# Key-value and mid-state products from hi and lo parts, with inner products between them and the state updates moved

## The reference

```
q, k, v, g = split(rms_norm(x) @ w_in); q, k = rotary(q), rotary(k) * 256 ** -0.5
scores = (q @ k.T) * decay_mask                  # within a chunk, causal
inner  = scores @ v
cross  = (q @ s_prev) * cross_decay              # s_prev: the state of the chunks before
kv     = (k * k_decay).T @ v                     # key-value product, 256 x 512
s_new  = gamma ** L * s_prev + kv                # for the prompt, and for each of 8 samples
o = group_norm(inner + cross)
x = x + (silu(g) * o) @ w_out
```

## Time and profile before

| | |
|---|---|
| median of 3 runs | 1457.37 us (1456.34 to 1457.72) |
| the profiled execution | 1458.02 us |
| its span in the profile | 1454.7 us |
| mean granted TensorE clock | 1.00 |
| TensorE busy | 1449.2 us, 100% |
| VectorE busy | 799.9 us, 55% |
| ScalarE busy | 543.2 us, 37% |
| GpSimd busy | 2.9 us |
| DMA | 171.94 MB, mean 118 GB/s |

### The profile page before, as it was taken

One profiled execution on the slowest core, in us unless ns is written; L12 is line 12 of the kernel. 1 busy time (PEld: TensorE's weight loads), 2 busy tenths in 40 slices (PEclk: granted clock), 3 DMA queues, 4 the chain that ended last, 5 costly groups with the idle time before them and its releaser, 6 DMA issues.

```text
span 1454.7 us, 27349 instructions
## 1 busy us (share of the span) xinstructions
PE 1449.2 (100%) x11428; PEld 1395.2 (96%) x11428; DVE 799.9 (55%) x1066; ACT 543.2 (37%) x776; POOL 2.9 (0%) x24
## 2 busy tenths in 40 slices
PE   9999999999999999999999999999999999999998
PEld 9699789879979999999999999999999999999998
DVE  7885577468458855555542427444565555553222
ACT  5552273264155543333331314222343333332222
POOL 0000000000000000000000000000000000000000
PEclk9999999999999999999999999999999999999999
DMA  8445253463444322222222222232223222222221
GB/s 302 149 186 192 96 225 107 180 232 104 166 162 178 115 89 87 89 98 87 87 93 100 87 88 88 88 97 92 89 89 100 87 87 99 88 87 101 92 88 59
DMA packets 47742, 171.94 MB, mean 118 GB/s; under 512 B 5608, under 2 KB 6248, under 8 KB 46624
## 3 DMA queue, kind: packets, MB, share of 16 engines
q1 hardware_dynamic: 47488, 170.76, 33.8%
q0 software_dynamic: 32, 0.03, 0.0%
q10 hardware_dynamic: 144, 0.00, 0.0%
HBM read 149.44 MB, written 21.55 MB: 118 GB/s over the span
## 4 chain that ended last, share of the span: by engine, by line
issue 100%; POOL 0%; POOLq 0%
POOLq L107 0%; POOL ident L266 0%; POOL h_tail L263 0%; POOL k_tail_stack L275 0%; POOL mean_v L259 0%; POOL ident L257 0%; POOL h_hi L261 0%; POOL h_lo L262 0%; POOL sample_ones L274 0%; POOL sample_ones L279 0%; POOL mean_d L258 0%; POOL late_q_decayed L276 0%; POOL seed L268 0%; POOL seed L269 0%; POOL seed L271 0%
## 5 line engine op out<-in xcount | busy, mean ns | idle before, releaser
L846 ACT ACTIVATE w_hi<-w_raw 128x1024 fp32r<-128x1024 f32 x227 | 240.1, 1059 | 671.4 <-PE ps L405 469.1
L405 PE MATMUL ps<-h_hi,w_hi 128*128 128x264 f32 (+2 forms) x2300 | 468.3, 285 | 0.4 <-DVE h_lo L1184 0.4
L405 PE MATMUL ps<-h_lo,w_hi 128*128 128x264 f32 (+2 forms) x2300 | 465.4, 284 | 0.0
L405 PE MATMUL ps<-h_hi,w_lo 128*128 128x264 f32 (+2 forms) x2300 | 464.9, 283 | 0.0
L1159 DVE TENSOR_TENSOR w_lo<-w_raw,w_hi 128x1024 fp32r<-128x1024 f32 x227 | 277.0, 1222 | 334.5 <-ACT w_hi L846 334.2
L405 PEld LDWEIGHTS ps<-h_hi,w_hi 128*128 128x128 f32 x2300 | 355.8, 188 | 1.5 <-issue 0.8
L405 PEld LDWEIGHTS ps<-h_hi,w_lo 128*128 128x128 f32 x2300 | 355.5, 188 | 0.0
L405 PEld LDWEIGHTS ps<-h_lo,w_hi 128*128 128x128 f32 x2300 | 355.3, 188 | 0.0
L695 PE MATMUL ps<-z_hi,w_lo 128*128 128x264 f32 (+1 forms) x704 | 144.7, 283 | 0.0
L695 PE MATMUL ps<-z_lo,w_hi 128*128 128x264 f32 (+1 forms) x704 | 144.6, 283 | 0.0
L695 PE MATMUL ps<-z_hi,w_hi 128*128 128x264 f32 (+1 forms) x704 | 144.6, 283 | 0.0
(11 more groups left out here) (205 smaller groups left out, 1407.7 us busy)
## 6 DMA issues: line engine op xcount, KB each, us to landing
w_raw<-in_w_units_dram SPq DMA_DIRECT2D x227, 512.0 KB, 3.3
states<-in_state_ret_dram SPq DMA_DIRECT2D x32, 512.0 KB, 8.5
out_ret_s_dram<-states SPq DMA_DIRECT2D x32, 512.0 KB, 4.6
v_bcast<-v_scratch SPq DMA_DIRECT2D x8, 1024.0 KB, 5.6
x_res<-in_x_all_dram SPq DMA_DIRECT2D x8, 268.0 KB, 6.0
out_ret_p_dram<-tmp SPq DMA_DIRECT2D x4, 512.0 KB, 3.7
out_y_prompt_dram<-y_rows SPq DMA_DIRECT2D x4, 512.0 KB, 2.6
decay<-in_decay_dram SPq DMA_DIRECT2D x4, 299.5 KB, 3.8
```

The costliest lines, as they stand in the source:

```text
L405: out = mm(PS[:, 2 * s + half, at:at + n_col], a, b[:, lo:lo + n_col], start=first and n == 0, stop=last and n == 2)
L846: fn(WH[:, c % NS, :], RAW[:, c % NR, :], ACT.Copy).then_inc(hi_ready, 1)
```

## The change

- The key-value products are computed from three fp32r products each. ACT writes the high part of V beside V (all four blocks, L1017 and L1018) and the high part of the keys (`k_rows_hi`); DVE subtracts to get both low parts (L1416, L1425, `k_rest`). DVE no longer scales two V blocks itself.
- The products of the late queries with the mid state become three fp32r products each. ACT copies the mid state's high part (`mid_hi`), DVE writes the low part (`mid_rest`), and the late queries are split likewise.
- TensorE's order: the mid sums for e = 0 and 1, then the early inner products of dt = 0, which wait for two score tiles, then the rest of the key-value products and the mid queries of dt = 0 by turns, then the late part of dt = 0, then dt = 1 to 3. Tile dt = 2 waits for the first of two additions that make up `KV`.
- The state updates, with ACT's outer products, move into the stages p = 1, 2, 3 of the output projection (2, 2 and 4 of them). Those of the last head move into the first two bodies of the FFN of layer 0.
- SP's list: the broadcast of V waits for the inner products and stands behind unit 14; the next head's units 0 to 5 come before or between the state stores. y_sample leaves from ACT instead of GpSimd.
- Some SBUF tiles lie over others: the mid state parts and the V parts in space that is free at that time, `KV` in the gate tile.

The diff, cut to what the text speaks of:

```diff
+UPDATES = ((), (0, 1), (2, 3), (4, 5, 6, 7))
+FFN_UPDATES = ((0, 1, 2, 3), (4, 5, 6, 7))
...
-                VB = sb("v_bcast", [P, NB, DV], scope=s3)
+                VH = sb("v_rows_hi", [P, 4, DV], F32R, scope=s3)
+                VL = sb("v_rows_lo", [P, 4, DV], F32R, scope=s3)
...
+            def store_state(h, b):
+                sp.wait_ge(s_upd, NB * h + (b + 1))
+                sp.dma_start(st_out[b, h], S[:, b, :]).then_inc(s_out[b], 16)
...
-                for b in range(NB):
-                    sp.wait_ge(s_upd, NB * h + (b + 1))
-                    sp.dma_start(st_out[b, h], S[:, b, :]).then_inc(s_out[b], 16)
-                for n in range(14, 16):
...
+                sp.wait_ge(v_sent, 16 * h + 16)
+                sp.wait_ge(inner_done, 4 * h + 4)
+                for half in range(2):
+                    b = half * NB // 2
+                    sp.dma_start(VB[:, b:b + NB // 2, :], VSCR[b:b + NB // 2, :].partition_broadcast(P)).then_inc(vb_in[half], 16)
+                in_heads(h, 15)
+                for n in range(4):
...
+                        ffn_in_unit(0, 1, n)
...
+                    for p in (1, 2):
+                        for b in UPDATES[p]:
+                            store_state(h, b)
+                        next_unit(h, 3 + p)
...
+                def key_value(e, js):
+                    for j in js:
+                        kh, kl = KNH[:, j, e * P:(e + 1) * P], KNL[:, j, e * P:(e + 1) * P]
+                        for q, (k, v) in enumerate(((kh, VH), (kh, VL), (kl, VH))):
+                            out = mm(PS[:, 6 + e, :], k, v[:, j, :], start=j in (0, 2) and q == 0, stop=j == 1 and q == 2)
+                    return out
+
+                for e in range(2):
+                    pe.wait_ge(kn_lo, 4 * h + 2 * e + 2)
+                    pe.wait_ge(v_lo, 4 * h + 4)
+                    key_value(e, (0, 1)).then_inc(mid_done, 1)
+
+                def key_value_end(e):
+                    pe.wait_ge(mid_lo, 2 * h + e + 1)
...
+                def early_values(dt):
+                    for j in range(2):
...
+                def mid_queries(dt, e):
+                    pe.wait_ge(ql_lo, 2 * h + e + 1)
+                    pe.wait_ge(mid_lo, 2 * h + e + 1)
+                    km = slice(e * DV + dt * P, e * DV + (dt + 1) * P)
+                    for q, (k, c) in enumerate(((KMH, QLH), (KMH, QLL), (KML, QLH))):
+                        mm(PS[:, 2 * INNER[dt] + 1, 0:N_LATE + NB], k[:, km], c[:, e, :], start=e == 0 and q == 0, stop=False)
...
+                pe.wait_ge(p_ready, 5 * h + 2)
+                pe.wait_ge(const_ready, QL_ZERO)
+                early_values(0)
+                key_value_end(0)
+                mid_queries(0, 0)
+                key_value_end(1).then_inc(kv_done, 1)
+                mid_queries(0, 1)
                 pe.wait_ge(p_ready, 5 * h + 5)
...
+                late_values(0).then_inc(inner_done, 1)
+                for dt in range(1, 4):
...
-                        pe.wait_ge(kv_ready, h + 1)
+                        pe.wait_ge(kv_sum, h + 1)
...
+                    early_values(dt)
                     for e in range(2):
...
+                        mid_queries(dt, e)
+                    late_values(dt).then_inc(inner_done, 1)
...
-                for b in (0, 2):
...
+                for b in range(4):
+                    if b < 3:
+                        act.wait_ge(v_acc, 3 * h + b + 1)
+                    else:
+                        act.wait_ge(unit_done, U_HEAD * h + (NS + 8))
                     fn(V[:, b, :], PS[:, 2 + b, :], ACT.Copy, scale=RN[:, b:b + 1]).then_inc(v_ready, 1)
...
+                    fn(VH[:, b, :], PS[:, 2 + b, :], ACT.Copy, scale=RN[:, b:b + 1]).then_inc(v_hi, 1)
...
-                    fn(KN[:, j, :], src, ACT.Copy, scale=DEC[:, DEC_ROW + j:DEC_ROW + j + 1]).then_inc(kn_ready, 1)
+                    fn(KNH[:, j, :], src, ACT.Copy, scale=DEC[:, DEC_ROW + j:DEC_ROW + j + 1]).then_inc(kn_ready, 1)
...
+                def mid_hi(e):
+                    act.wait_ge(mid_done, 2 * h + e + 1)
+                    fn(KMH[:, e * DV:(e + 1) * DV], PS[:, 6 + e, :], ACT.Copy).then_inc(mid_ready, 1)
+
+                mid_hi(0)
+                for e in range(2):
+                    act.wait_ge(ql_ready, 2 * h + e + 1)
+                    fn(QLH[:, e, 0:N_LATE], QT[:, e, :], ACT.Copy).then_inc(ql_hi, 1)
+                mid_hi(1)
...
-                for e in range(2):
-                    act.wait_ge(mid_done, 2 * h + e + 1)
-                    fn(KM[:, e * DV:(e + 1) * DV], PS[:, 6 + e, :], ACT.Copy).then_inc(mid_ready, 1)
...
+                    if not last:
+                        for b in UPDATES[p]:
+                            outer(h, b)
...
+            act.wait_ge(ys_out, 1)
+            act.dma_start(io["y_sample"], YS[:].rearrange("p k b -> p (k b)")).then_inc(ys_sent, 16)
...
+            def update(h, b):
+                dve.wait_ge(samp_kv, 16 * h + (2 * b + 2))
+                at = (b % 2) * 1024
+                stt(S[:, b, :], S[:, b, :], DEC[:, DEC_STATE:DEC_STATE + 1], G[:, at:at + 1024], ALU.mult, ALU.add).then_inc(s_upd, 1)
...
-                dve.wait_ge(v_acc, 3 * h + 2)
-                ts(V[:, 1, :], PS[:, 3, :], RN[:, 1:2], None, ALU.mult).then_inc(v_some, 1)
...
+                for b in range(4):
+                    dve.wait_ge(v_ready, 5 * h + b + 2)
+                    dve.wait_ge(v_hi, 4 * h + b + 1)
+                    tt(VL[:, b, :], V[:, b, :], VH[:, b, :].bitcast(F32), ALU.subtract).then_inc(v_lo, 1)
+                    if b < 2:
+                        dve.wait_ge(v_tail, 4 * h + 4)
+                        tt(QT[:, b, :], Q[:, b, CUT:TP], DEC[:, DEC_Q:DEC_ROW], ALU.mult).then_inc(ql_ready, 1)
...
+                def k_rest(j):
+                    if j % 2 == 0:
+                        dve.wait_ge(kn_ready, 4 * h + j + 2)
+                    src = PS[:, 6 + j // 2, (j % 2) * DK:(j % 2 + 1) * DK]
+                    stt(KNL[:, j, :], src, DEC[:, DEC_ROW + j:DEC_ROW + j + 1], KNH[:, j, :].bitcast(F32),
+                        ALU.mult, ALU.subtract).then_inc(kn_lo, 1)
+
+                k_rest(0)
+                k_rest(1)
...
+                k_rest(2)
+                k_rest(3)
...
+                def mid_rest(e):
+                    dve.wait_ge(mid_ready, 2 * h + e + 1)
+                    mid = slice(e * DV, (e + 1) * DV)
+                    tt(KML[:, mid], PS[:, 6 + e, :], KMH[:, mid].bitcast(F32), ALU.subtract).then_inc(mid_lo, 1)
+
+                mid_rest(0)
...
+                for e in range(2):
+                    dve.wait_ge(ql_hi, 2 * h + e + 1)
+                    tt(QLL[:, e, 0:N_LATE], QT[:, e, :], QLH[:, e, 0:N_LATE].bitcast(F32), ALU.subtract).then_inc(ql_lo, 1)
+                mid_rest(1)
...
-                tt(KV, PS[:, 6:8, :].rearrange("p e v -> p (e v)"), KM, ALU.add).then_inc(kv_ready, 1)
...
+                tt(KV, PS[:, 6:8, :].rearrange("p e v -> p (e v)"), KMH[:].bitcast(F32), ALU.add).then_inc(kv_sum, 1)
+                dve.wait_ge(kv_sum, h + 1)
+                tt(KV, KV, KML[:].bitcast(F32), ALU.add).then_inc(kv_ready, 1)
...
-                dve.wait_ge(s_upd, NB * h + NB)
+                dve.wait_ge(kv_sent, 16 * h + 16)
...
+                    if not last:
+                        for b in UPDATES[p]:
+                            update(h, b)
...
-                body(0, True)
-                with dve.Fori(1, JF // 2) as i:
+                body(0, True, FFN_UPDATES[0] if l == 0 else ())
+                if l == 0:
+                    body(1, False, FFN_UPDATES[1])
```

More of the change, by code:

```diff
@@ L325, in _, with ffn_in_unit, next_unit, head @@
             sp.dma_start(CF[:], io["ffn_consts"]).then_inc(ffn_in, 16)
-            def head(h, first):
-                for n in range(4 if first else 0, 6):
-                    in_heads(h, n)
+            def ffn_in_unit(l, i, n):
+                load(U_FFN_IN[l] + 4 * i + n)
+            def next_unit(h, n):
+                if h < HEADS - 1:
+                    in_heads(h + 1, n)
+                else:
+                    ffn_in_unit(0, 0, n)
+            def store_state(h, b):
+                sp.wait_ge(s_upd, NB * h + (b + 1))
+                sp.dma_start(st_out[b, h], S[:, b, :]).then_inc(s_out[b], 16)
+            def head(h, first, last):
+                def load_state(b):
+                    if not first:
+                        sp.wait_ge(s_out[b], 16 * h)
+                    sp.dma_start(S[:, b, :], st_in[b, h]).then_inc(s_in[b], 16)
+                if first:
+                    for n in range(4, 6):
+                        in_heads(h, n)
                 if first:
@@ L1460, in body @@
                         dve.wait_ge(ff_hi, 2 * i + (JF + 8) * l)
+                    for b in samples:
+                        update(HEADS - 1, b)
                     dve.wait_ge(unit_done, 4 * i + (u0 + NS + 2))
```

192 lines of the change are left out of this document (88 added, 104 removed).

## The result

The changed kernel takes 1448.40 us (median of 6 runs, 1448.32 to 1448.62), the kernel before 1457.24 (6 runs). The ratio is 0.9941, interval 0.9930 to 0.9951. It is faster by 8.8 us; 1449.7 was forecast, 7.7 less, with a range of 1448.0 to 1453.8.

What follows compares the result with a forecast made beforehand. TensorE, busy 1449.2 of 1454.7 us, was taken as the bound. Shorter products -8.1, stall +0.6 and tail -0.2 gave -7.7 from the 1457.37 median: 1449.7 us, range 1448.0 to 1453.8.

Steps and rivals of the forecast that it cites:

- TensorE's sum: Key-value and mid-query products in the heads: 10.68 us becomes 8.66, so 2.02 less a head, 8.1 in four.
- The chain through the mid state: TensorE waits for the mid state's low part: stall 0.6 us in head 0, none in heads 1 to 3.
- The sign named for it: In the profile after, TensorE's waits should list DVE's mid_state_lo with about 0.6 us, mostly in head 0.
- rival B: Mid-state chain late in every head, 0.6 to 1.6 us more in each of four: 1452.1 to 1456.1; chance 0.16.
- The updates moved: State updates moved into output projection and FFN fit in DVE's idle time: cost 0.
- SP's queue: Reordered V broadcast, unit loads, state stores and loads still arrive in time: cost 0.
- Rival C: States' update, store and load end late, the sample fold delays TensorE: 1460.3 us and more; chance 0.03.
- Rival D: No change: DVE late at the z chain returns 2 us a head, 1455 to 1458; chance 0.06.
- The tail: y_sample's transfer leaving from ACT at the end saves 0.2 us, between 0 and 0.67.

Runs made afterwards that it cites:

- a_early_late: Changed kernel with early values of tile 0 (0.64 us) placed behind the rest of the key-value products for e = 0; 1450.36 us.
- a_all32: Changed kernel with key-value and mid-query products as single fp32 products again (rounded parts, low parts not read); 1456.45 us, 0.9996 of before.
- a_upd3: Changed kernel with all eight state updates of heads 0 to 2 behind the split of p = 3; 1448.45 us.
- a_upd1: Changed kernel with all eight state updates of heads 0 to 2 behind the split of p = 1; 1460.47 us.
- a_pool: Changed kernel with y_sample's transfer issued by GpSimd again; 1448.52 us.
- b_act: Kernel before with only y_sample's transfer moved to ScalarE; 1456.87 us against 1456.92.
- a_same: The changed kernel itself, measured again as reference in a later series; 1448.57 us, 0.9942 of before.
- b_gap: Kernel before with only the unused 888-column tile added between z_hi and z_lo of the FFN; 1456.13 us against 1457.02.
- v_late: Changed kernel with late scores x V products (272 and 144 columns) also from three fp32r products each; 1448.91 us.
- v_j2: v_late with the mid state's high and low parts for e = 0 made earlier and the 144-column product single fp32 again; 1447.68 us.

## Why the prediction was right

**TensorE's sum** was right: 2.02 us in a head was forecast, 1.96 came (head 1), and the two halves apart measured 5.1 and 3.0 against 5.2 and 2.9 in four heads. The price of an fp32r product of 280 columns, which no row showed, is 0.129; 0.128 was taken, from a line between two rows. The formula of the Trainium skill, page "TensorE: Matmul & The Clock Gate", section "Back-to-back issue gap", would have given 0.119 and 0.216; the trace has 0.129 and 0.232, so it does not agree, by 7 to 8%. The page has this formula for matmuls back to back, but the section named calls it the gap of an isolated one and gives 0.131 for 512 columns in a sustained stream, from which the trace is further off.

**The chain through the mid state** was right in its place (head 0 alone, TensorE just late) and too long by 0.3: stall 0.26 instead of 0.6. The sign named for it, a row of `mid_state_lo` among TensorE's waits, did not appear, since the stall was too short. The steps held. The operations ahead of mid_rest were each a few hundredths cheaper in a row than the printed durations that the prediction had used, and the block from the second score product on took 67.38 - 65.21 = 2.17 instead of 2.33; mid_rest itself took 0.69 instead of 0.66. 68.8 on the clock of before was forecast for the end of mid_rest, and it came at 68.07 + 0.29 = 68.36. In heads 1 to 3 the cover of 0.2 was 0.3 to 0.4, and rival B had nothing: `a_early_late` shows that 0.64 us less cover costs 0.34 to 0.37 in each.

**The updates moved** cost nothing, as forecast, and `a_all32` and `a_upd3` show it by themselves. `a_upd1` shows that "nothing" holds for the pair at p = 1, not for any number.

**SP's queue**: no transfer among TensorE's waits. Rival C was excluded with over 5 us to spare. Rival D had no ground: in head 1 the first z_lo ended at 220.99 and TensorE wanted it at 223.20, 2.2 us of cover instead of 0.45.

**The tail** was the one term that had no ground: 0.2 taken for ScalarE's issue of y_sample, nothing measured (`a_pool`, `b_act`).

**Not in the forecast** was the place of z_lo, 0.6 us, though the line of the unused tile stood in the full diff. I had read it as a matter of room. With it, the smaller stall (0.3) and no gain in the tail (0.2), -7.7 becomes -8.4, and with the 7.84 that the four heads gave instead of 8.1 it is -8.2. The median moved by 8.3 (`a_same`) to 8.8, depending on the series. It is luck that the sizes which were off within the sum cancel in part: the stall was taken 0.3 too long, the heads' gain 0.3 and the tail's 0.2 too large.

## What to carry to other kernels

Where one engine is busy without a gap, price a replaced instruction by the distance of starts in its own stream, not by its printed duration, and the forecast of its part was good to a few per cent here (2.02 against 1.96). Two fp32 records are worth replacing by three fp32r products while these stay clear of their floor of 0.11 us: here at 512, 280 and 272 columns yes, at 144 no. When a hand-over between engines is new, look for independent work of the waiting engine to put ahead of it: here two products of 0.64 us were worth 1.7 us in four heads.

## What the runs showed of the hardware

- An unused tile in front of z_lo in SBUF changed TensorE's mean distance of starts by 0.3 to 0.8 ns in 121 (`b_gap`), the same to 0.01 us of the stage in every execution that was profiled.
- After a wait of 2.7 us TensorE had a stretch at a granted clock of 0.50 (1.2 GHz) in two heads out of three (`a_upd1`): in head 0 its products slowed down 1.7 us after the wait, in head 2 at once. Each cost some 1.5 us more. In `a_early_late` no such stretch followed the wait of 0.7 us.
- fp32r products with 144 columns cost some 0.115 each (`v_late` against `v_j2`), although 264 columns take only 0.121; with 272 it is 0.125, with 280 0.129, with 512 0.232.
- What lies outside the profile's span took 1.7 to 3.3 us for one and the same kernel (that before). The stretch up to head 0's V products took 33.1 to 34.3 us over all profiles. Differences under a microsecond between two profiled executions have to be read stage by stage.
